# First block of a two-block transformer kernel: stages put in another order, and the context's modulation sums moved from VectorE to GpSimd

## The chip, the cores and the metric

The kernel runs on one core of a Trainium2 chip. The metric is the device time of one execution in microseconds (us). It is one program of about 20,900 instructions; nothing is exchanged with other cores.

## What is computed

Two blocks of a small transformer on 256 tokens of width 1024, all in float32. The first block has two layers; each projects x, forms two attentions (one with low-rank queries and keys, one differential), gates and merges them, and normalises. The second block has half feed-forward sublayers, one windowed attention with a context and one Fourier mixer, and all of them are modulated by vectors that depend only on the inputs `c`, `c_ctx` and `mod_w`:

```python
h = x @ w_in[l]                                   # first block, layer l
y_a = (o_a * silu(gate_a)) @ w_branch_a[l]
y_b = (rms_norm(o_b) * (1 - lam_init) * silu(gate_b)) @ w_branch_b[l]
g = sigmoid(gates + b_merge[l])
merged = g[..., :D] * y_a + g[..., D:] * y_b
x = layer_norm(ALPHA * x + merged @ w_out[l])

mod_lat = silu(c) @ mod_w[i] + mod_b[i]           # second block, sublayers' shift, scale, gate
mod_ctx = silu(c_ctx) @ mod_w[i] + mod_b[i]       # the same for the context, i = 0 only
x = layer_norm(ALPHA * x + gate * y)
```

## The kernel before

**Products in float32.** Every weight piece (128 x 1024, one half of a 1 MB load into one of five raw slots) is split in two: ScalarE writes the rounded part `w_hi` (L1124), VectorE the rest `w_lo` = raw - `w_hi` (`split`, L1488). TensorE multiplies three times for each product (L579 to L581). The activations are split likewise: TensorE transposes, ScalarE writes `xT_hi`, VectorE `xT_lo`. `w_hi` has six slots, so ScalarE and VectorE run at most five to six pieces ahead of TensorE. A piece is 12 matmuls of 128x512 for two token tiles. All order is written by hand: each engine has its own program, and counts in semaphores tie them together. What stands first in an engine's program runs first.

**The first block's layer.** On TensorE: transpose x, ten chunks of `w_in` (the low-rank columns, gate A, then four chunks, later four for the gates), low-rank products, eight heads with one gate piece each, four differential heads with two, the transposes of the gated values, the products with `w_branch_a` and `w_branch_b` (two column halves each, in the banks acc0 to acc3), the transposes of their merged sum, `w_out` in two halves, the second by token tile (`project_by_tile`). VectorE follows with splits, rotations, maxima, gates, and at the end `layer_norm`, which updates, centres and scales tile 0 and then tile 1. `keep_busy(b, n)` issues n needless matmuls (two instructions each, L698) that write a free bank; `turn(..., wait=(5, 10))` puts them ahead of the transposes of each tile.

**The modulation.** The vectors are computed beside this, in chunks of 512 columns. GpSimd's queue loads `mod_w` into a ring of two slots of two features each, `mod_raw` (`mod_load`, L479; four loads a chunk). VectorE multiplies each feature by its `silu` column and adds it to a running sum over eight features (`mod_feature`, L1607 for the first and L1609 for the others). In the first block a chunk is done twice, once for the latents into `mod_sum_lat` (counter `mod_step`) and, in five of six chunks a layer, once for the context into `acc_ctx` (`ctx_step`). TensorE sums over the partitions with `mod_sum` into bank score1, and VectorE's `mod_store` (L1626, L1627) adds the bias and frees the bank. `split_and_mod(n, features)` interleaves n splits with the features. A load waits until VectorE has used the slot before.

**The merge.** VectorE does, for each branch and each half: two splits with a feature, then `products(2)` (wait for TensorE's pieces), then the two gate products (L1815), which free the banks; for the second branch then the sum of both (L1820) and `merged_ready`, one for each half.

**Second block.** `post_norm` multiplies the product by the row `gate_row`. That row is fetched by `gate_load`, which writes the vector of 1024 to DRAM, element by element so that it lies in the order of the columns, and reads it back to all partitions. `project_first` starts a feed-forward by token tile, with `keep_busy` where nothing else is to be done. In `attention`, `pairs` transposes queries and keys through two banks.

Of the kernel before, what the change touches and what calls it, by code (L numbers as in the profile page):

```python
# [21 lines left out]
F32R = mybir.dt.float32r  # L22
# [4 lines left out]
P = 128  # L27
TOK = 256
# [46 lines left out]
MOD_RING = 2  # L75
N_GATES = 7
MOD_KEPT = 3 * D // 512
KEPT_EARLY = 2
SUM_COLS = 48

# [10 lines left out]
FIRST_SPLITS, HEAD_MORE = 1, (1, 3, 5)  # L91
# [45 lines left out]
def program(nc, a, out):  # L137
    with ExitStack() as ctx:
# [19 lines left out]
        x = sb("x", [P, NT, D])  # L158
        xT_hi = sb("xT_hi", [P, KD, TOK], F32R)
        xT_lo = sb("xT_lo", [P, KD, TOK], F32R)  # L160
        mod_raw = sb("mod_raw", [P, MOD_RING, 2, 512])
# [34 lines left out]
        first = ExitStack()  # L196
        scope[0] = first
        low = sb("low", [P, NT, LOW])
        wide = sb("wide", [P, NT, WIDE])
        work = sb("work", [P, 3072])  # L200
        v_a = sb("v_a", [P, NT, HEADS * DV])
        qkT = sb("qkT", [P, 2 * HEADS, TOK])
        qkdT = sb("qkdT", [P, 2 * DHEADS, TOK])
        cT_hi = sb("cT_hi", [P, 3, TOK], F32R)
        cT_lo = sb("cT_lo", [P, 3, TOK], F32R)
        lam_sum = sb("lam_sum", [P, LAYERS * 2])
        low_sq = sb("low_sq", [P, 4])
        low_inv = sb("low_inv", [P, 4])
        row_max = sb("row_max", [P, HEADS, 4])
        neg_max = sb("neg_max", [P, HEADS, 4])  # L210
        row_sum = sb("row_sum", [P, HEADS, 4])
        row_inv = sb("row_inv", [P, HEADS, 4])
        diff_sq = sb("diff_sq", [P, DHEADS * NT])
        diff_inv = sb("diff_inv", [P, DHEADS * NT])
        mod_sum_lat = sb("mod_sum_lat", [P, 512])
        acc_ctx = sb("acc_ctx", [P, 2, 512])
        first.close()

# [10 lines left out]

        second = ExitStack()  # L230
        scope[0] = second
        ctx_area = sb("ctx_area", [P, 2 * 2 * FHALF + NT * 3 * TOK + 12])
        ctx_x = ctx_area[:, 0:NT * D].rearrange("p (t n) -> p t n", t=NT)
        gate_row = sb("gate_row", [P, D])
        turned_more = sb("turned_more", [P, 2, 512])
        gated = sb("gated", [P, NT, D])
        ffn_scope = second.enter_context(ExitStack())
        scope[0] = ffn_scope
        hT_hi = sb("hT_hi", [P, KF, TOK], F32R)
        hT_lo = sb("hT_lo", [P, KF, TOK], F32R)  # L240
        silu_g = sb("silu_g", [P, 2, NT, FC])
        hidden = sb("hidden", [P, 2, NT, FC])
        mod_kept = sb("mod_kept", [P, MOD_KEPT, 512])
        ffn_scope.close()
        att_scope = second.enter_context(ExitStack())
        scope[0] = att_scope
        qkv = sb("qkv", [P, NT, QKV])
        ctx_kv = sb("ctx_kv", [P, NT, 2 * AKV * AD])
        qkv_bias = sb("qkv_bias", [P, QKV])
        ctx_scope = att_scope.enter_context(ExitStack())  # L250
        scope[0] = ctx_scope
        ctxT_hi = sb("ctxT_hi", [P, KD, TOK], F32R)
        ctxT_lo = sb("ctxT_lo", [P, KD, TOK], F32R)
        ctx_scope.close()
        scope[0] = att_scope
        qT = sb("qT", [P, AH // 2, TOK])
        kT = sb("kT", [P, AKV, 2 * TOK])
        band = sb("band", [P, NT, 2 * TOK])
        att_work = sb("att_work", [P, 8 * 512])
        att_max = sb("att_max", [P, AH, NT])  # L260
        att_neg = sb("att_neg", [P, AH, NT])
        att_sum = sb("att_sum", [P, AH, NT])
        att_inv = sb("att_inv", [P, AH, NT])
        sink_exp = sb("sink_exp", [P, AH, NT])
        att_scope.close()
        scope[0] = second
# [1903 lines left out]
```

## Time and profile before

| | |
|---|---|
| median of 3 runs | 1677.95 us (1675.96 to 1678.39) |
| the profiled execution | 1674.37 us |
| its span, first to last instruction | 1672.7 us |
| granted TensorE clock, mean | 0.989 of full |
| busy in the span: TensorE, its weight loads, VectorE, ScalarE, GpSimd | 95%, 79%, 72%, 48%, 8% |
| loads of `mod_w` | 144 of 512 KB, median 6.0 us from issue to landing |
| loads of `b_merge` | 4 of 1024 KB, median 10.1 us |

Times in the profile are in us from the start of the span. A busy TensorE is a model, since its matmuls overlap: 128x512 matmuls are shown with 0.39 us each and start 0.23 us apart. An idle time is put down to the instruction that ended it. "L1609" is a line of the kernel.

### The profile page before, as it was taken

To read this page: it belongs to the slowest core of one execution; us is meant where nothing else is said; L and a number is where in the kernel's file an instruction comes from. 1 tells how busy PE (TensorE), PEld (TensorE's weight loads), DVE (VectorE), ACT (ScalarE), POOL (GpSimd) and SP (SyncE) were. 2 spreads that over 40 slices of the span, in tenths; PEclk is the share of its full clock that TensorE was granted. 3 is DMA by queue.
4 is the path that set the end of the run, shared out by engine and by line. 5 is a ranking of instruction groups with operands and counts; after the bars stand their busy time and mean duration, and the time that the engine had idled before them with its cause. 6 is when DMAs were issued, how large, how long until landed. Compare 5 with 4: busy or idle time off the path is not lost.

```text
span 1672.7 us, 20900 instructions
## 1 busy us (share of the span) xinstructions
PE 1596.4 (95%) x7847; PEld 1318.7 (79%) x7847; DVE 1200.0 (72%) x1847; ACT 794.8 (48%) x1241; POOL 140.3 (8%) x205
## 2 busy tenths in 40 slices
PE   6999989999889999999999799999999999999997
PEld 6887768887778878888888458887888878888876
DVE  6888887987977776777756867777587775566544
ACT  4565534566434444444535465444354443264442
POOL 1100001100001110011100011111001110000000
PEclk9999999999999999999999999999999999999999
DMA  7864357753468877588658205987668866366552
GB/s 266 307 220 154 138 178 267 246 181 132 163 209 263 273 263 246 180 272 284 239 198 240 71 1 181 289 283 266 213 227 278 272 225 232 89 193 195 179 177 76
DMA packets 200509, 349.64 MB, mean 209 GB/s; under 512 B 11188, under 2 KB 128236, under 8 KB 199900
## 3 DMA queue, kind: packets, MB, share of 16 engines
q1 hardware_dynamic: 174668, 252.90, 46.5%
q0 software_dynamic: 25744, 95.43, 16.3%
q8 instruction: 63, 1.03, 0.3%
q14 instruction: 34, 0.28, 0.1%
HBM read 347.21 MB, written 1.08 MB: 208 GB/s over the span
## 4 chain that ended last, share of the span: by engine, by line
PE 82%; DVE 12%; ACT 2%; DMA 2%; issue 1%; SPq 0%; DVEq 0%; ACTq 0%
PE acc L579 24%; PE acc L581 24%; PE acc L580 24%; DVE w_lo L1488 3%; PE turn L923 1%; PE score L706 1%; DMA raw<-in_attn_wqkv 1%; PE acc L831 1%; PE score L1009 1%; DVE x L1589 1%; DVE att_work L2040 1%; DMA raw<-in_w_in 1%; DVE acc_ctx L1609 1%; PE score L718 1%; PE score L698 1%
## 5 line engine op out<-in xcount | busy, mean ns | idle before, releaser
L1488 DVE TENSOR_TENSOR w_lo<-raw,w_hi 128x1024 fp32r<-128x1024 f32 (+2 forms) x490 | 581.4, 1196 | 286.2 <-ACT w_hi L1124 285.2
L1124 ACT ACTIVATE w_hi<-raw 128x1024 fp32r<-128x1024 f32 (+2 forms) x490 | 503.5, 1040 | 505.1 <-PE acc L581 420.8
L579 PE MATMUL acc<-w_hi,xT_hi 128*128 128x512 f32 (+1 forms) x1440 | 573.0, 398 | 17.5 <-DVE wide L1738 6.6
L581 PE MATMUL acc<-w_hi,xT_lo 128*128 128x512 f32 (+1 forms) x1440 | 563.5, 391 | 0.0
L580 PE MATMUL acc<-w_lo,xT_hi 128*128 128x512 f32 (+1 forms) x1440 | 562.6, 391 | 0.0
L579 PEld LDWEIGHTS acc<-w_hi,xT_hi 128*128 128x128 f32 x1440 | 272.3, 189 | 74.0 <-issue 8.4
L581 PEld LDWEIGHTS acc<-w_hi,xT_lo 128*128 128x128 f32 x1440 | 272.2, 189 | 57.2
L580 PEld LDWEIGHTS acc<-w_lo,xT_hi 128*128 128x128 f32 x1440 | 272.5, 189 | 53.1
L479 POOL DMA_DIRECT2D mod_raw<-in_mod_w x144 | 104.3, 724 | 951.9 <-DVE mod_run L1609 758.3
L579 PE MATMUL acc<-w_hi,hT_hi 128*128 128x512 f32 x440 | 174.3, 396 | 0.1
L581 PE MATMUL acc<-w_hi,hT_lo 128*128 128x512 f32 x440 | 173.6, 395 | 0.0
L580 PE MATMUL acc<-w_lo,hT_hi 128*128 128x512 f32 x440 | 173.6, 395 | 0.0
L1609 DVE SCALAR_TENSOR_TENSOR mod_run<-mod_raw,silu_c,mod_run 128x512 f32<-128x512 f32 x216 | 161.2, 746 | 3.8 <-DMA mod_raw<-in_mod_w 3.8
L579 PEld LDWEIGHTS acc<-w_hi,hT_hi 128*128 128x128 f32 x440 | 82.8, 188 | 20.5 <-DVE hT_lo L1950 1.3
L581 PEld LDWEIGHTS acc<-w_hi,hT_lo 128*128 128x128 f32 x440 | 82.8, 188 | 19.5
L580 PEld LDWEIGHTS acc<-w_lo,hT_hi 128*128 128x128 f32 x440 | 82.8, 188 | 19.1
L1355 ACT ACTIVATE silu_g<-acc 128x256 f32<-128x256 f32 x110 | 36.2, 381 | 82.3 <-PE acc L581 82.3
L1188 ACT ACTIVATE turned<-x,neg_mean 128x1024 bf16<-128x1024 f32 x16 | 18.5, 1157 | 85.3 <-DVE neg_mean L1578 85.3
L1609 DVE SCALAR_TENSOR_TENSOR acc_ctx<-mod_raw,silu_c,acc_ctx 128x512 f32<-128x512 f32 x70 | 52.2, 746 | 3.0 <-DMA mod_raw<-in_mod_w 2.9
L1943 DVE TENSOR_TENSOR hidden<-acc,silu_g 128x256 f32<-128x256 f32 x110 | 41.6, 420 | 12.0 <-ACT silu_g L1355 8.1
L1264 ACT ACTIVATE work<-score,neg_max 128x256 f32<-128x256 f32 x64 | 29.6, 472 | 30.5 <-DVE neg_max L1716 30.5
L1950 DVE TENSOR_TENSOR hT_lo<-turn,hT_hi 128x512 fp32r<-128x512 f32 x55 | 38.1, 692 | 3.8 <-ACT hT_hi L1359 3.5
(278 smaller groups left out, 1335.8 us busy)
## 6 DMA issues: line engine op xcount, KB each, us to landing
raw<-in_ffn_wi SPq DMA_DIRECT2D x220, 512.0 KB, 4.9
mod_raw<-in_mod_w POOLq DMA_DIRECT2D x144, 512.0 KB, 6.0
raw<-in_ffn_wo SPq DMA_DIRECT2D x110, 512.0 KB, 4.5
raw<-in_w_in SPq DMA_DIRECT2D x72, 512.0 KB, 7.2
raw<-in_w_out SPq DMA_DIRECT2D x16, 512.0 KB, 4.7
raw<-in_attn_wqkv SPq DMA_DIRECT2D x16, 512.0 KB, 4.7
wide<-in_b_merge POOLq DMA_DIRECT2D x4, 1024.0 KB, 10.1
raw<-in_w_branch_a SPq DMA_DIRECT2D x8, 512.0 KB, 4.6
```

What stands on the lines that cost most here:

```text
L479: pool.dma_start(mod_raw[:, s, :, :], w_mod[l, :, 2 * i:2 * i + 2, at]).then_inc(mod_in[s], 16)
L579: nc.tensor.matmul(dst, xh, wh, start=start, stop=False)
L580: nc.tensor.matmul(dst, xh, wl, start=False, stop=False)
L581: return nc.tensor.matmul(dst, xl, wh, start=False, stop=stop)
L1124: nc.scalar.activation(piece_part(w_hi[:, i % SPLIT_SLOTS, :], i), piece_part(raw[:, s, i % 2 * PIECE:(i % 2 + 1) * PIECE], i), ACT.Copy). ...
L1188: step(nc.scalar.activation(squares[:, t, :], x[:, t, :], ACT.Square, bias=neg_mean[:, t:t + 1], accum_out=square_sum[:, t:t + 1]))
L1264: m = nc.scalar.activation(p[:, t * TOK:t * TOK + TOK], bank[b][:, t * TOK:t * TOK + TOK], ACT.Exp, bias=neg_max[:, h, 2 * m_ + t:2 * m_ + ...
L1355: nc.scalar.activation(silu_g[:, half, t, :], bank[ACC[2 * half + t]][:, FC:2 * FC], ACT.Silu).then_inc(silu_done, 1)
L1488: nc.vector.tensor_tensor(piece_part(w_lo[:, i % RAW_PIECES, :], i), piece_part(raw[:, i // 2 % RAW_SLOTS, i % 2 * PIECE:(i % 2 + 1) * PIE ...
L1609: m = nc.vector.scalar_tensor_tensor(out=end if k == KD - 1 else run, in0=w, scalar=by, in1=run, op0=ALU.mult, op1=ALU.add)
L1943: nc.vector.tensor_tensor(hidden[:, half, t, :], bank[b][:, 0:FC], silu_g[:, half, t, :], ALU.mult).then_inc(moved[b], 1)
L1950: nc.vector.tensor_tensor(sl(hT_lo), bank[b][:], sl(hT_hi).bitcast(F32), ALU.subtract).then_inc(moved[b], 1)
```

## The change

It reorders work of the first block and of the attention, moves buffers within SBUF, and moves one kind of work to another engine.

- The context's features: GpSimd multiplies the loaded weights in place (`tensor_scalar`) and adds them to the running sum (`tensor_tensor`), each followed by a wait for its own end. It does this behind VectorE, which must have read the feature first. A slot is reloaded behind GpSimd's own features. GpSimd's loop over the layers is written out, and the rows and biases of the layer are loaded before the fifth load of the ring, which is now behind the features of the third.
- The merge: products first, splits behind them; the last gate products and the last sum by token tile, with `by_tile` on TensorE's side; the transposes of the merged halves wait separately.
- The layer's end: features in other places, `mod_store` of the fourth chunk ahead of the first early splits, that of the fifth in the wait for the root of the second tile.
- `move_gates` stands ahead of the feature in the heads and ahead of the maxima in the differential heads; `HEAD_MORE` is (1, 4, 5) for (1, 3, 5).
- Fewer `keep_busy`: (0, 6) for (5, 10), and 2, 8, 2 for 6, 11, 6.
- The attention: four banks for the pairs, splits moved behind the copies of the keys and to the last heads, two waits in GpSimd's queue ahead of the loads of the band and of the rows.
- The gate vector is written to DRAM contiguously by partition, and `gate` reads the row with a step of eight elements.

```diff
-FIRST_SPLITS, HEAD_MORE = 1, (1, 3, 5)
+FIRST_SPLITS, HEAD_MORE = 1, (1, 4, 5)
+BRANCH_FEATURES = [(3, 4), (5, 6), (7,), ()]
...
+            def ctx_feature(k):
+                s = k // 2 % MOD_RING
+                if k % 2 == 0:
+                    pool.wait_ge(mod_in[s], 16 * c.next(f"mod_in{s}"))
+                pool.wait_ge(mod_step, c.next("feature") + 2 * MOD_RING)
+                w, by = mod_raw[:, s, k % 2, :], silu_c[:, C_CTX + k:C_CTX + k + 1]
+                if k == 0:
+                    nc.gpsimd.tensor_scalar(acc_ctx[:, 0, :], w, by, None, ALU.mult).then_inc(ctx_step, 1)
+                    pool.wait_ge(ctx_step, c.next("ctx"))
+                    return
+                nc.gpsimd.tensor_scalar(w, w, by, None, ALU.mult).then_inc(ctx_part_ready, 1)
+                pool.wait_ge(ctx_part_ready, c.next("part"))
+                if k == KD - 1:
+                    if c.now("ctx chunk"):
+                        pool.wait_ge(ctx_stored, c.now("ctx chunk"))
+                    c.next("ctx chunk")
+                nc.gpsimd.tensor_tensor(acc_ctx[:, k // (KD - 1), :], w, acc_ctx[:, 0, :], ALU.add).then_inc(ctx_step, 1)
+                pool.wait_ge(ctx_step, c.next("ctx"))
+            def chunk_loads(chunks, behind_first):
+                loads = [(ctx_too, at, i) for ctx_too, at in chunks for i in range(4)]
+                for q in range(len(loads) + MOD_RING):
+                    if q >= MOD_RING:
+                        ctx_too, _, i = loads[q - MOD_RING]
+                        if ctx_too:
+                            for k in (2 * i, 2 * i + 1):
+                                ctx_feature(k)
+                        else:
+                            c.next(f"mod_in{i % MOD_RING}")
+                            c.next("feature", 2)
+                    if q == 4:
+                        behind_first()
+                    if q < len(loads):
+                        _, at, i = loads[q]
+                        s = i % MOD_RING
+                        pool.wait_ge(mod_step, 2 * c.next("mod load"))
+                        pool.dma_start(mod_raw[:, s, :, :], w_mod[0, :, 2 * i:2 * i + 2, at]).then_inc(mod_in[s], 16)
...
+            pool.wait_ge(k_twice_ready, 1)
             pool.dma_start(band[:], a["band"].rearrange("(t p) n -> p t n", p=P)).then_inc(band_in, 16)
+            pool.wait_ge(exps_ready, 1)
             norm_rows(a["ln_g_2"][0, 1], a["ln_b_2"][0, 1])
...
-                after = turn(lambda t, k: x[:, t, k * P:k * P + P], x_tile, wait=(5, 10))
+                after = turn(lambda t, k: x[:, t, k * P:k * P + P], x_tile, wait=(0, 6))
...
+                        if by_tile and t == 0 and i == pieces - 1:
+                            m.then_inc(first_done, 1)
...
-                    split_and_mod(HEAD_PIECES[h], ((h + 3) % KD,), True)
+                    split(HEAD_PIECES[h])
+                    move_gates(HEAD_PIECES[h])
+                    mod_feature((h + 3) % KD)
...
+                for n in range(2):
+                    products(2)
+                    for t in range(NT):
+                        gate_branch(0, n, t)
+                    split_and_mod(2, BRANCH_FEATURES[n])
+                products(2)
+                for t in range(NT):
+                    gate_branch(1, 0, t)
+                dve.wait_ge(moved["acc1"], c.next("acc1 moved", 13) + 1)
+                for t in range(NT):
+                    m = merge(0, t)
+                m.then_inc(merged_ready, 1)
+                split_and_mod(1, BRANCH_FEATURES[2])
+                for t in range(NT):
+                    if t == 0:
+                        dve.wait_ge(first_done, c.next("first"))
+                    else:
                         products(2)
+                    b = ACC[2 + t]
+                    gate_branch(1, 1, t)
+                    dve.wait_ge(moved[b], c.next(b + " moved", 11 - 4 * t) + 1)
+                    merge(1, t).then_inc(merged_ready, 1)
                 c.next("acc1 moved")
                 turn_plain(xT_hi, xT_lo, scale=0.5)
-                split_and_mod(2, range(0, 4), True)
-                mod_store(*ctx_chunk(3))
-                split_and_mod(1, range(4, 6), True)
+                split_and_mod(3, BRANCH_FEATURES[3])
+                split_and_mod(2, range(0, 4))
+                split_and_mod(1, range(4, 7))
...
+                mod_store(*ctx_chunk(3))
                 split(EARLY)
-                for k in (6, 7):
-                    mod_feature(k, True)
-                layer_norm(update, lambda t: wide[:, t, 0:D], between=split)
-                mod_store(*ctx_chunk(4))
+                mod_feature(7)
+                layer_norm(update, lambda t: wide[:, t, 0:D], between=split, at_root=lambda: mod_store(*ctx_chunk(4)))
                 mods_stored()
...
-                    nc.vector.scalar_tensor_tensor(out=gated[:, t, at], in0=bank[b][:], scalar=factor, in1=gate_row[:, at],
+                    by_chunk = lambda r: r.rearrange("q (k p) -> q k p", p=P)
+                    row = gate_row[:].rearrange("q (p k) -> q k p", k=KD)[:, 4 * n:4 * n + 4, :]
+                    nc.vector.scalar_tensor_tensor(out=by_chunk(gated[:, t, at]), in0=by_chunk(bank[b][:]), scalar=factor, in1=row,
                                                    op0=ALU.mult, op1=ALU.mult).then_inc(moved[b], 1)
```

## Rows read from the trace of the kernel before

**Rows 1.** Busy time in the first layer; columns: PE, PEld, DVE, ACT, POOL, clock, DMA
```profile
21.68:257.68 236.00, 219.42 (x1159) 187.43 (x1159) 193.84 (x356) 120.20 (x229) 19.53 (x28) 0.97 0.59 198
```
**Rows 2.** TensorE's waits in the whole span: us in total, times, longest
```profile
PE score L600 <- DVE mod_lat L1627: 8.6, 2, 4.4
PE acc L579 <- DVE wide L1738: 6.6, 4, 2.0
...
PE score L600 <- DVE wide L1820: 5.7, 2, 3.6
...
PE acc L579 <- DVE wide L1815: 4.2, 2, 2.1
```
**Rows 3.** Timeline of TensorE behind the merge: start, us, line, operation, [idle before]
```profile
221.12 0.63 PE L580 MATMUL acc<-w_lo,xT_hi 128*128 128x512 f32 x1
221.55 0.53 PE L581 MATMUL acc<-w_hi,xT_lo 128*128 128x512 f32 x1
221.91 0.39 PE L579 MATMUL acc<-w_hi,xT_hi 128*128 128x512 f32 x1
222.15 0.40 PE L580 MATMUL acc<-w_lo,xT_hi 128*128 128x512 f32 x1
```
**Rows 4.** Timeline of TensorE at the end of the first layer
```profile
243.51 0.99 PE L706 MATMUL score<-ones,mod_sum_lat 128*128 128x48 f32 x8
...
251.55 0.44 PE L600 MATMUL score<-ident,x 128*128 128x128 f32 x2 [4.18 <-DVE mod_lat L1627]
251.83 3.81 PE L698 MATMUL acc<-ones,ident 128*128 128x128 f32 x20
255.43 0.87 PE L600 MATMUL turn<-ident,x 128*128 128x128 f32 x4
...
257.68 0.43 PE L579 MATMUL acc<-w_hi,xT_hi 128*128 128x416 f32 x1
```
**Rows 5.** Timeline of VectorE at the end of the first layer
```profile
247.29 0.68 DVE L1833 SCALAR_TENSOR_TENSOR x<-x,acc 128x512 f32<-128x512 f32 x1
...
250.07 1.28 DVE L1589 SCALAR_TENSOR_TENSOR x<-wide,inv_std,ln_rows 128x1024 f32<-128x1024 f32 x1
```
**Rows 6.** Timeline of VectorE in the attention, behind the keys
```profile
935.54 3.49 DVE L1488 TENSOR_TENSOR w_lo<-raw,w_hi 128x1024 fp32r<-128x1024 f32 x3
```
**Rows 7.** Timeline of TensorE: first pairs of the attention; filler of `project_first`
```profile
935.68 3.44 PE L991 MATMUL turn<-ident,qkv 128*128 128x128 f32 x16 [3.67 <-DVE gated L2014]
...
1028.06 2.62 PE L698 MATMUL score<-ones,ident 128*128 128x128 f32 x22
```
**Rows 8.** VectorE's groups in the first layer: count, busy us, mean ns, idle before
```profile
L1488 DVE TENSOR_TENSOR w_lo<-raw,w_hi 128x1024 fp32r<-128x1024 f32 (+3 forms) x64 | 70.6, 1115 | 6.9 <-ACT w_hi L1124 6.6
...
L1609 DVE SCALAR_TENSOR_TENSOR acc_ctx<-mod_raw,silu_c,acc_ctx 128x512 f32<-128x512 f32 x35 | 26.1, 746 | 2.5 <-DMA mod_raw<-in_mod_w 2.5
...
L1607 DVE TENSOR_SCALAR acc_ctx<-mod_raw,silu_c 128x512 f32<-128x512 f32 x5 | 2.4, 483 | 2.8 <-DMA mod_raw<-in_mod_w 2.8
```
**Rows 9.** GpSimd's arithmetic by line: duration in ns, least, median, most
```profile
L530 POOL TENSOR_TENSOR xT_lo<-gated,xT_hi x8: 727/732/740, 959.7 to 1006.0; 128x256 fp32r<-128x256 f32 x8
...
L528 POOL CAST xT_hi<-gated x8: 392/398/1323, 959.2 to 1004.6; 128x256 fp32r<-128x256 f32 x8
```
**Rows 10.** Timeline of GpSimd's queue: biases, then the fifth load of the ring
```profile
36.51 1.11 POOL L506 DMA_DIRECT2D wide<-in_b_merge  x2
...
41.14 0.72 POOL L479 DMA_DIRECT2D mod_raw<-in_mod_w  x1 [2.48 <-DVE mod_run L1609]
```
**Rows 11.** Timeline of VectorE: the first feature of the second chunk
```profile
54.90 0.49 DVE L1607 TENSOR_SCALAR acc_ctx<-mod_raw,silu_c 128x512 f32<-128x512 f32 x1 [2.76 <-DMA mod_raw<-in_mod_w]
```
**Rows 12.** Timeline of TensorE: `mod_sum` of the second chunk
```profile
78.75 0.99 PE L706 MATMUL score<-ones,mod_sum_lat 128*128 128x48 f32 x8
```
**Rows 13.** Timelines of VectorE and GpSimd where both read SBUF
```profile
1004.47 1.22 DVE L1488 TENSOR_TENSOR w_lo<-raw,w_hi 128x1024 fp32r<-128x1024 f32 x1
...
1004.62 1.32 POOL L528 CAST xT_hi<-gated 128x256 fp32r<-128x256 f32 x1 [4.03 <-DVE gated L2066]
```

More of the change, by code:

```diff
@@ new lines, in program @@
+        mod_sum_lat = sb("mod_sum_lat", [P, 512])
+        acc_ctx = sb("acc_ctx", [P, 2, 512])
+        first.close()
+        scope[0] = ctx
+        second = ExitStack()
+        scope[0] = second
+        ffn_scope = second.enter_context(ExitStack())
+        scope[0] = ffn_scope
+        hT_hi = sb("hT_hi", [P, KF, TOK], F32R)
+        hT_lo = sb("hT_lo", [P, KF, TOK], F32R)
+        silu_g = sb("silu_g", [P, 2, NT, FC])
+        hidden = sb("hidden", [P, 2, NT, FC])
+        mod_kept = sb("mod_kept", [P, MOD_KEPT, 512])
@@ L227, in program @@
         rot = turned[:, 0:2, 0:HEADS * ROPE]
[L230 to L266, printed above, removed]
-        xmT = sb("xmT", [P, KD, TOK])
-        spectrum = sb("spectrum", [P, NT, FGROUPS, 2 * FHALF])
-        second.close()
         dft_ch = ctx_area[:, 0:4 * FHALF].rearrange("p (k n) -> p k n", k=2)
@@ L672, in project_by_tile, with project @@
                         m.then_inc(first_done, 1)
-            def project(banks, pieces, k0=0, n=512, after=None, xh=xT_hi, xl=xT_lo, ready=None):
+            def project(banks, pieces, k0=0, n=512, after=None, xh=xT_hi, xl=xT_lo, ready=None, by_tile=False):
                 dst = [take(b) for b in banks]
@@ L890, in _ @@
                 diff_values(DHEADS - 1)
+                after = turn(lambda t, k: wide[:, t, GATE_A + k * P:GATE_A + k * P + P], groups=range(2))
                 mod_sum(True)
-                after = turn(lambda t, k: wide[:, t, GATE_A + k * P:GATE_A + k * P + P], groups=range(2))
                 project(ACC[0:2], 2, k0=0, after=after)
@@ L1097, in fourier @@
                 project_by_tile(ACC[2:4])
-            after = turn_x(wait=(5, 10))
+            after = turn_x(wait=(0, 6))
             keep_busy("acc0", 5)
@@ new lines, in merge @@
+                def merge(n, t):
+                    of = lambda branch: wide[:, t, GATES + branch * D + n * 512:GATES + branch * D + n * 512 + 512]
+                    return nc.vector.tensor_tensor(of(0), of(0), of(1), ALU.add)
+                for n in range(2):
[6 more added lines that the diff above has]
+                    gate_branch(1, 0, t)
@@ L2034, in attention @@
                         c.next(b)
+                split()
                 def maxima(h):
```

205 lines of the change are left out of this document (114 added, 91 removed).

## Prediction

> **What bounds the kernel now.** I read the page first: TensorE is busy 95% of the span, so a gain can come only from stretches where it stands or runs slowly. The window of the first block's first layer [rows 1] shows where they are: of 236.0 us TensorE is busy 219.4, VectorE 193.8 (82%), GpSimd 19.5. Next the list of TensorE's waits [rows 2]: the four entries that the change touches are all on VectorE and all in the first block: 8.6 + 6.6 + 5.7 + 4.2 = 25.1 us over the two layers. The half-feed-forward stages of the second block hardly appear in that list, and the change leaves their order alone. So the question is the first block and, less, the attention.
>
> Then the timelines. In the merge of the two branches TensorE waits for `wide` L1815, because VectorE does two splits and two features ahead of the product that frees the bank, and for `wide` L1820 at the end. Behind such a wait its matmuls start 0.43 us apart instead of 0.23, at the lower of the two clocks (1.2 GHz): [rows 3] show the end of such a stretch. At the end of a layer [rows 4] TensorE waits 4.18 us for `mod_lat` L1627 (the bank score1, which `mod_store` empties only behind the layer norm), then runs 20 filler instructions for 3.81 us although `x` was ready at 251.35 [rows 5], and resumes real work at 257.68.
>
> **The reordering, part by part.** (1) Merge. `products` and the gate products now stand ahead of the splits, so the wait for L1815 goes: 4.2 us. The last gate products go tile by tile with `by_tile`; tile 0 is finished while TensorE is still on tile 1 (six matmuls of 0.23, 1.4 us), so behind the last matmul only one gate product and one sum are left, about 1.3 us, of which 1.0 lies beside transposes. I leave 0.45 us of each of the two waits for L1820: 5.7 - 0.9 = 4.8 us. The cold stretch has about nine matmuls at 0.2 us extra, 1.8 us, and comes once in each layer: 3.6 us. Sum 12.6.
>
> (2) Ends of layers. VectorE loses features ahead of the first update, which is queued behind them now. TensorE has the first tile finished at about 238.0 (half of its 48 matmuls of 0.23 before 243.5), so that update can begin there; the second tile's update cannot begin before the last matmul at 243.5, it begins at 247.29 now, so `x` is ready about 3.8 us sooner, at 247.5. `mod_store` moves into the wait for the root, so score1 is free in time. The filler ahead of the second tile falls from 20 instructions to 12 (1.6 us at full clock) and ends near 247.8. From the transposes of the second tile (255.43) to the resumption (257.68) is 2.25 us [rows 4]; 247.8 + 2.25 = 250.05 against 257.68 is 7.6 us. The other layer end has the same wait (8.6 less 4.18 is 4.4) and the same fillers; I take 7.5 there, 15.1 in all. At the very start the same fillers are cut, but there ScalarE waits for weights, so I count nothing.
>
> (3) Attention. One split ahead of the rotation of the keys goes away, and two of three behind it [rows 6]: 3.49/3 = 1.16 each, 3.5 us in a chain on which TensorE waits 3.67 [rows 7] and again further on. Four banks for the pairs instead of two add nothing, ScalarE and VectorE empty them at the old pace. The wait put ahead of the band's load holds GpSimd, and behind it the rows of the norm and the gate; the band's 512 KB then arrive about when the first maxima want them, so I take 2.5 of the 3.5. With `project_first` the filler falls from 12 and 22 instructions to 4 and 16, and 12 to 4; it stands ahead of transposes whose input is ready, and 22 of it take 2.62 us [rows 7]: some 0.9 us twice in each of two calls, 3.6. Sum 6.1.
>
> (4) Heads. 6.6 us of waits for `wide` L1738 [rows 2]: `move_gates` now precedes the feature and the extra split of head 3 goes to head 4. All of it could go; with GpSimd on the same memory I take 2.
>
> (5) The gate vector goes to DRAM contiguously, and `gate` reads its row with a step of eight elements. The cheaper transfer is hidden already. What the stepped read costs VectorE no row shows: between nothing and doubling a 0.7 us instruction (the sum of 512 elements of [rows 5] is 0.68), some eight of them with nothing beside them, 0 to 5 us. I take 0, the second input being one of two and the first from PSUM, and keep 5 for the range.
>
> Together 12.6 + 15.1 + 6.1 + 2 = 35.8 us. The moves of buffers in SBUF cost nothing by themselves.
>
> **GpSimd's features.** Off VectorE come, per layer, 35 instructions of 0.746 and five of 0.483, 26.1 + 2.4 = 28.5 us of the 193.8 [rows 1, 8]. On GpSimd each becomes a multiply and an add of 128x512. The trace has its cast and add at 128x256, 0.40 and 0.73 us [rows 9]; a feature is thus between 1.13 (if size cost nothing) and 2.26 (double). The step from the cast to the add shows that time per element matters more than a fixed part, so I stay near double, 2.0: 35 x 2.0 + 5 x 0.7 = 73.5 us per layer, on an engine busy for 19.5 of 236. In itself that fits. Two things don't come free.
>
> First the ring of two slots. A slot is now reloaded only when VectorE and then GpSimd have read it, and GpSimd works in place. Now the loads of the biases go out at 36.5 and the fifth load at 41.14 [rows 10], and VectorE gets it at 54.90, after a wait of 2.76 [rows 11]: these transfers are already late. In the change the biases stand behind GpSimd's features of the third load, which VectorE cannot touch before some 38; with 4 us for two features and a lag, they go out at about 43 to 44, and the first feature of the second chunk comes at 60 to 62. VectorE's splits stand in order behind it; TensorE has a lead of about two pieces there, so it is caught once. Then a slot's turn is load 6.5 (the page's median for it is 6.0, and these stretches are crowded) + VectorE 2.5 + GpSimd 2.5 = 11.5 for two pairs of features, 5.75 each, where TensorE asks for a pair in 5.5 (two pieces of 12 matmuls of 0.23), hence no catching up, and `mod_sum(True)`, which TensorE reaches at 78.75 [rows 12], must wait for GpSimd's last add near 83 to 85. I price this at 5 to 8 us per layer, 6.5 taken: 13 for the two. The bounds are 0 (the load lands as before) and 12 per layer.
>
> Second the memory port. One pair of rows speaks of it: VectorE's split, both inputs in SBUF, starts at 1004.47 for 1.22; GpSimd's cast starts at 1004.62 and lasts 1.32 instead of 0.40, ending 0.25 after the split [rows 9, 13]. So GpSimd stands while VectorE has such an instruction. Whether VectorE stands for GpSimd no row shows. I take a little, 3 us in all, because in the dense stretches both read all the time.
>
> The Trainium skill (SBUF — State Buffer, section Who interferes with whom) says that a VectorE instruction with two SBUF inputs and a GpSimd instruction that reads SBUF exclude one another, whichever starts second blocking for the whole of the other. [Rows 13] agree for the one direction. By that rule the other direction holds too, and the sum would be that of rival B below.
>
> Sum: 35.8 - 13 - 3 = about 20 us. The profiled execution took 1674.4 (span 1672.7, 1.7 around it), 3.6 below the median of the runs shown, 1677.95. 1674.4 - 20 is 1654.4 there, and 1658 on the median's level: I forecast 1657.
>
> **Rivals.** A: GpSimd's work is free, its loads come in time: -36, that is 1642. For it: GpSimd is idle 90% and TensorE's lead is five pieces; against it: [rows 10, 11]. Chance 0.20. B, slower: VectorE pays for GpSimd's port. Per layer VectorE then has 193.8 - 28.5 + 73.5 = 238.8 us against 236.0 for the whole layer now, and it still has to wait for TensorE and ScalarE at least 10 us: 249 per layer, 13 more than now, times two is 26, less 6 for attention: 20 slower, 1698. It decides from the point where VectorE's paid time reaches about half of GpSimd's 73.5: there a layer needs 202 + 20 to 30 of dependency waits and the gain of the reordering is used up. For it: the splits and the latents' 40 or more features, two SBUF inputs each, are 70.6 and some 30 us per layer [rows 8]; against it: a third of VectorE's work reads PSUM, and only one direction is seen. Chance 0.19, half of it below 1690. C: the stalls move from the ends of layers to the ring one for one, 12 per layer and port 9: within 0.2%, or 3 us, of now. Chance 0.07. The forecast's own case, 1646 to 1668, has 0.54.
>
> **Numbers.** Likeliest case 1657, its own range 1646 to 1668. For 8 in 10: down to A's 1640, up into B's lower half, with the 5 us of the stepped read, 1688. Faster by over 0.2% (3.4 us, about what a measurement can tell from no change): 0.54 + 0.20 = 0.74; same 0.07; slower 0.19.
>
> **What would show it.** In the changed trace: no wait of TensorE for the gate product of `wide` (now L1815), under 1 us for the merged sum (now L1820); a layer end that resumes about 7 us after the last `mod_sum`; a new wait of TensorE for `acc_ctx` or for a split early in each layer, and of VectorE for `mod_raw` there. If VectorE's splits are longer than 1.22 us, or its instructions start late, while GpSimd is at a feature, B holds. Splits of constant length and GpSimd's instructions stretched in places mean that only GpSimd pays. The prediction is wrong if a feature takes GpSimd over 3 us, or if VectorE is blocked for over 20 us per layer.

## The result: 57 us slower, and where they are in the profile after

The changed kernel takes 1734.37 us (1734.28 to 1737.24, 4 runs) against 1677.72 (1675.96 to 1678.39, 4 runs): ratio 1.0343, 95% interval 1.0326 to 1.0361. The forecast was 1657. Times of experiments below are medians; the kernel before had medians of 1675.1 to 1678.5 beside them.

The page of the kernel after, its busy line and its clock by slices (in tenths of full speed):

```profile
span 1732.6 us, 20738 instructions
...
PE 1603.5 (93%) x7749; PEld 1330.3 (77%) x7749; DVE 1211.7 (70%) x1766; ACT 794.6 (46%) x1241; POOL 403.8 (23%) x355
...
PEclk9889988889988999999999999999999999999999
```

Start with the stage. VectorE's last scaling of x in the first block, then the last of all, in the kernel before (its own rows, not among those above):

```profile
484.15 1.28 DVE L1589 SCALAR_TENSOR_TENSOR x<-wide,inv_std,ln_rows 128x1024 f32<-128x1024 f32 x1
...
1668.34 1.28 DVE L1589 SCALAR_TENSOR_TENSOR x<-gated,inv_std,ln_rows 128x1024 f32<-128x1024 f32 x1
```

and in the kernel after:

```profile
555.69 1.29 DVE L1651 SCALAR_TENSOR_TENSOR x<-wide,inv_std,ln_rows 128x1024 f32<-128x1024 f32 x1
...
1728.25 1.29 DVE L1651 SCALAR_TENSOR_TENSOR x<-gated,inv_std,ln_rows 128x1024 f32<-128x1024 f32 x1
```

The first block ends 71.5 us later; from there to the end it is 1172.6 us against 1184.2, so 11.6 us sooner. The whole loss is in the first block, where the modulation runs. TensorE's waits there are new:

```profile
PE score L767 <- POOL acc_ctx L529: 34.5, 3, 12.0
PE score L767 <- issue: 26.2, 3, 9.5
PE turn L657 <- DVE wide L1873: 10.5, 2, 5.3
...
PE score L657 <- DVE wide L1873: 6.8, 4, 2.3
```

Six times in ten chunks TensorE stands some 10 us in front of `mod_sum`, 60.7 us in all. The first two lines are one cause: "issue" is a wait for which no releaser is recorded, and the timeline has GpSimd's last addition right before it. TensorE's and then GpSimd's rows, second chunk of the first layer:

```profile
95.06 1.91 PE L767 MATMUL score<-ones,mod_sum_lat 128*128 128x48 f32 x8 [9.53 <-issue]
```

```profile
64.13 2.97 POOL L520 TENSOR_SCALAR acc_ctx<-mod_raw,silu_c 128x512 f32<-128x512 f32 x1 [4.61 <-DVE mod_run L1665]
...
70.98 0.76 POOL L551 DMA_DIRECT2D mod_raw<-in_mod_w  x1 [0.30 <-POOL acc_ctx L529]
71.79 2.01 POOL L523 TENSOR_SCALAR mod_raw<-mod_raw,silu_c 128x512 f32<-128x512 f32 x1
73.89 1.28 POOL L529 TENSOR_TENSOR acc_ctx<-mod_raw,acc_ctx 128x512 f32<-128x512 f32 x1
75.27 1.57 POOL L523 TENSOR_SCALAR mod_raw<-mod_raw,silu_c 128x512 f32<-128x512 f32 x1
76.92 2.05 POOL L529 TENSOR_TENSOR acc_ctx<-mod_raw,acc_ctx 128x512 f32<-128x512 f32 x1
79.27 0.76 POOL L551 DMA_DIRECT2D mod_raw<-in_mod_w  x1 [0.30 <-POOL acc_ctx L529]
...
87.48 0.76 POOL L551 DMA_DIRECT2D mod_raw<-in_mod_w  x1 [0.30 <-POOL acc_ctx L529]
...
93.39 1.57 POOL L529 TENSOR_TENSOR acc_ctx<-mod_raw,acc_ctx 128x512 f32<-128x512 f32 x1
```

GpSimd never rests here for more than 0.3 us: one load and two features take it 8.3 and 8.2 us. TensorE wants two features in 5.5. The last addition ends at 94.96 and TensorE goes on at 95.06. It comes back at the lower clock: the granted clock is 1.00 in the 5 us ahead of the wait and 0.50 in the 5 us behind it, and the eight small matmuls take 1.91 us, 0.99 in [rows 12]. Over the stretch of [rows 1] the granted clock is 0.91 now instead of 0.97.

VectorE stands for the same reason on the other side, since a slot is reloaded only behind GpSimd. Its waits for `mod_raw`:

```profile
DVE mod_run L1667 <- DMA mod_raw<-in_mod_w: 78.5, 21, 9.1
...
DVE mod_run L1665 <- DMA mod_raw<-in_mod_w: 25.1, 4, 11.5
```

Where both engines work, GpSimd holds VectorE up in a second way. GpSimd's rows, then VectorE's:

```profile
45.30 1.56 POOL L523 TENSOR_SCALAR mod_raw<-mod_raw,silu_c 128x512 f32<-128x512 f32 x1
46.95 1.34 POOL L529 TENSOR_TENSOR acc_ctx<-mod_raw,acc_ctx 128x512 f32<-128x512 f32 x1
```

```profile
46.39 0.75 DVE L1667 SCALAR_TENSOR_TENSOR mod_run<-mod_raw,silu_c,mod_run 128x512 f32<-128x512 f32 x1 [3.98 <-DMA mod_raw<-in_mod_w]
47.06 2.31 DVE L1550 TENSOR_TENSOR w_lo<-raw,w_hi 128x1024 fp32r<-128x1024 f32 x1
```

The feature begins inside GpSimd's multiplication and takes its usual 0.75 us; the split begins inside the addition and takes 2.31 us instead of 1.22. The first block's timeline has the same throughout, counted over its rows of one instruction. Of 29 features and splits that begin inside an addition, 26 are longer, by 0.97 us on average; the other three begin in its last 0.06 us. Of 67 that begin inside a multiplication, 53 keep their length, and the others grow by 0.43 us at most.

### The profile page after: what moved, and what is told of

It reads as the page before. It is cut to its first block, busy times and chain, and to the rows that moved or that the text cites. A ratio compares the mean times of both kernels' runs of the same rounds, so it can differ in the third digit from the quotient of the medians.

```text
span 1732.6 us, 20738 instructions
## 1 busy us (share of the span) xinstructions
PE 1603.5 (93%) x7749; PEld 1330.3 (77%) x7749; DVE 1211.7 (70%) x1766; ACT 794.6 (46%) x1241; POOL 403.8 (23%) x355
## 4 chain that ended last, share of the span: by engine, by line
PE 68%; DVE 7%; POOL 5%; DMA 1%; ACT 1%; issue 1%; POOLq 0%; DVEq 0%; ACTq 0%
PE acc L636 20%; PE acc L638 20%; PE acc L637 20%; POOL mod_raw L523 2%; POOL acc_ctx L529 2%; PE turn L986 1%; DVE w_lo L1550 1%; DMA mod_raw<-in_mod_w 1%; DVE gated L1971 1%; PE score L779 1%; PE score L1072 1%; DVE att_work L2115 1%; PE score L767 1%; PE acc L892 1%; DVE x L1977 1%
## 5 line engine op out<-in xcount | busy, mean ns | idle before, releaser
L1550 DVE TENSOR_TENSOR w_lo<-raw,w_hi 128x1024 fp32r<-128x1024 f32 (+2 forms) x490 | 591.1, 1213 | 267.5 <-ACT w_hi L1187 267.0
L1667 DVE SCALAR_TENSOR_TENSOR mod_run<-mod_raw,silu_c,mod_run 128x512 f32<-128x512 f32 x216 | 180.3, 835 | 78.8 <-DMA mod_raw<-in_mod_w 78.5
L490 POOL DMA_DIRECT2D mod_raw<-in_mod_w x96 | 69.4, 723 | 536.0 <-DVE mod_run L1667 434.1
L523 POOL TENSOR_SCALAR mod_raw<-mod_raw,silu_c 128x512 f32<-128x512 f32 x70 | 131.6, 1880 | 134.3 <-DVE mod_run L1667 125.0
L529 POOL TENSOR_TENSOR acc_ctx<-mod_raw,acc_ctx 128x512 f32<-128x512 f32 x70 | 104.8, 1498 | 5.8
L638 PEld LDWEIGHTS acc<-w_hi,hT_lo 128*128 128x128 f32 x440 | 82.6, 188 | 17.3
L767 PE MATMUL score<-ones,mod_sum_lat 128*128 128x48 f32 x96 | 17.4, 340 | 60.7 <-POOL acc_ctx L529 34.5
L767 PEld LDWEIGHTS score<-ones,mod_sum_lat 128*128 128x128 f32 x96 | 16.7, 260 | 63.2 <-issue 63.1
```

The source lines that it names most:

```text
L490: pool.dma_start(mod_raw[:, s, :, :], w_mod[l, :, 2 * i:2 * i + 2, at]).then_inc(mod_in[s], 16)
L523: nc.gpsimd.tensor_scalar(w, w, by, None, ALU.mult).then_inc(ctx_part_ready, 1)
L529: nc.gpsimd.tensor_tensor(acc_ctx[:, k // (KD - 1), :], w, acc_ctx[:, 0, :], ALU.add).then_inc(ctx_step, 1)
L638: return nc.tensor.matmul(dst, xl, wh, start=False, stop=stop)
L767: m = nc.tensor.matmul(dst[:, 4 * i + j:4 * i + j + SUM_COLS], acc[:, j * P:j * P + P], ones[:, 0:SUM_COLS], start=True, stop=True)
L1550: nc.vector.tensor_tensor(piece_part(w_lo[:, i % RAW_PIECES, :], i), piece_part(raw[:, i // 2 % RAW_SLOTS, i % 2 * PIECE:(i % 2 + 1) * PIE ...
```

## Experiments: which half of the change it is

**Each half alone.** E1 is the changed kernel with `mod_feature(k, True)` back on VectorE; E2 is the kernel before with only the context's features and their loads on GpSimd.

```diff
-                split_and_mod(8, range(8))            # E1, and so for every call
+                split_and_mod(8, range(8), True)
```

> The changed kernel with the context's features back on VectorE; the order, the fillers, the banks, the places of the buffers and the gate row stay as changed. Theory W (GpSimd's features cost the time, because loads, VectorE's features and the partition sum wait for them; the reordering does what was forecast): 1640 to 1650, TensorE's waits for the partition sum gone. Rival R (a good part of the 57 us comes from the reordering itself, such as the fillers cut or the stepped read of the gate row): 1665 or more.

> The kernel before with one thing changed: the context's features of the first block on GpSimd, with the loads behind them, as in the change. Theory W: slower than before by 80 to 100 us (the 57 of the change plus some 35 that the reordering gives), 1760 to 1775. Rival R: 1700 to 1735, since then the two halves add up the other way.

E1: 1649.62 us, ratio 0.983 (0.981 to 0.985), 27 us faster than before. E2: 1752.21, ratio 1.044 (1.042 to 1.046). The move to GpSimd costs 75 us alone and 84.8 on top of the reordering; the reordering gives 27, not 35.8. E2 lies between its two expectations, so the halves do not simply add: on top of the move the reordering is worth only 18 us (1752.2 less 1734.4). E2 has the same waits at `mod_sum` in the old order, six with 58.0 us in all, so they come from the move and not from the reordering.

**Waits or sizes.** E3 keeps every instruction, wait and load and lets GpSimd work on 32 of the 512 columns. E4 keeps the sizes, takes `acc_ctx` as the only data and issues each load ahead of the features, so that no slot waits for GpSimd.

```diff
-                nc.gpsimd.tensor_scalar(w, w, by, None, ALU.mult).then_inc(ctx_part_ready, 1)
+                nc.gpsimd.tensor_scalar(w[:, 0:32], w[:, 0:32], by, None, ALU.mult).then_inc(ctx_part_ready, 1)
```

> The changed kernel with GpSimd's multiplies and adds on 32 of the 512 columns; the rest of the context's modulation is left out. All waits, counts and the order of the queue stay. Theory W, with the duration as its cause: about as the first kernel of this call, 1640 to 1655, and VectorE's wait for loads under 20 us in the block. Rival S (the chain of semaphores, loads behind features, whatever their duration): over 1690. Theory P (VectorE pays for GpSimd's port) can't be told from W here.

> The changed kernel with GpSimd's features at full size, but reading and writing only acc_ctx instead of the loaded weights (so the context's modulation is not computed), and each load issued ahead of the features of the load before last. The loads no longer wait for GpSimd to finish with a slot. If the ring is the cause (reload behind GpSimd): VectorE's waits for mod_raw fall from 104 us to under 40 and the time to about 1670. If GpSimd's rate is the cause (over 3 us a feature against 2.7 us a piece): the sums still wait about 10 us each and the time stays above 1700.

E3: 1649.08 us (two runs), as E1. With a quick GpSimd the 85 us are gone, though every semaphore, shared slot and late load is still there, and TensorE's waits at `mod_sum` fall from 60.7 to 0.7 us. The chain is not free for all that. VectorE still waits 58.6 us for `mod_raw`, where under 20 were expected, and E3 only equals E1, although it has taken the context's features off VectorE; E13 below shows some 17 us that this could give. E4: 1710.4 (two runs, 1705.8 and 1715.0), 24.0 less than the changed kernel, with 51.6 us of waits at `mod_sum` left: mostly the rate, and the ring has its share. With two runs 9 us apart, the 24.0 is known to a few us only.

**Nobody waits for the sums.** E6 is E4 without TensorE's wait; TensorE sums `mod_sum_lat` twice instead.

```diff
-                if ctx_too:
-                    pe.wait_ge(ctx_step, c.next("ctx mod", 8))
```

> The run with other data (1710.4 us), and now nobody waits for GpSimd's sums: TensorE's mod_sum doesn't wait for them and sums mod_sum_lat a second time in place of acc_ctx. GpSimd issues the same instructions on the same amount of data; the context's modulation is not computed. Theory W (GpSimd is too slow for the dense chunks, TensorE waits for its last addition): the 51.6 us of waits at mod_sum go, 1658 to 1670. Theory P (VectorE pays for the shared memory port): the time hardly falls, 1690 or more.

1685.55 us (1681.2 to 1689.9, 10 runs). The 51.6 us of waits are gone and 24.8 us are gained. Neither theory alone: 36 us above E3 remain, in which nobody waits for a result of GpSimd.

**The port.** This is short for whatever makes VectorE and GpSimd wait for each other when both read SBUF. E10 is E6 with GpSimd about as long at a feature but on 32 columns at a time; E13 is E6 with memsets, which write and read nothing.

```diff
+                for m in range(3):                    # E10, the multiply; the add twice
+                    o = nc.gpsimd.tensor_scalar(part(m), part(m), by, None, ALU.mult)
```

> The run in which nobody waits for GpSimd (1685.6 us), with each 128x512 multiply replaced by three of 128x32 and each add by two of 128x32: GpSimd is as long at a feature (3 x 0.84 + 2 x 0.37 = 3.3 us by the run with 32 columns) but moves less than a quarter of the data. The context's modulation is not computed. Theory P (what is left against the run with 32 columns, 36 us, is VectorE blocked by GpSimd's large accesses: its features took 0.97 us there and 0.75 here): 1648 to 1655, and VectorE's features at 0.75. Theory Q (it is GpSimd's time at a feature, behind which its queue issues the loads late): 1675 to 1690.

> The run in which nobody waits for GpSimd (1685.6 us), with each multiply and each add replaced by two memsets of 128x512, which write SBUF and read nothing. The context's modulation is not computed. Theory R (only instructions of GpSimd that read SBUF exclude VectorE): VectorE's features stay at 0.75 us while GpSimd is busy, 1648 to 1660. Theory X (writes exclude it as well): VectorE's features at 0.9 or more, above 1665 if the memsets take GpSimd as long.

VectorE's latent features in the first 500 us, in E6, E10 and E13 in turn (count, busy us, mean ns, idle before):

```profile
L1663 DVE SCALAR_TENSOR_TENSOR mod_run<-mod_raw,silu_c,mod_run 128x512 f32<-128x512 f32 x72 | 69.7, 968 | 40.0 <-DMA mod_raw<-in_mod_w 39.7
```

```profile
L1664 DVE SCALAR_TENSOR_TENSOR mod_run<-mod_raw,silu_c,mod_run 128x512 f32<-128x512 f32 x72 | 54.5, 757 | 51.7 <-DMA mod_raw<-in_mod_w 51.4
```

```profile
L1661 DVE SCALAR_TENSOR_TENSOR mod_run<-mod_raw,silu_c,mod_run 128x512 f32<-128x512 f32 x80 | 59.8, 748 | 18.4 <-DMA mod_raw<-in_mod_w 18.1
```

E10: 1668.56 us, between the theories. VectorE's features fall from 968 to 757 ns, 15.2 us over these 72, and 17.0 us are gained. That gain is not VectorE's price at the port alone, for GpSimd is also 46 us shorter in all (203 against 249). What is left against E13 would be GpSimd's own time, with its queue late with the loads; that is argued, not shown, for VectorE's waits for `mod_raw` do not follow the times: 58.6 us in E3, 65.2 in E6, 75.6 in E10, 28.9 in E13. GpSimd in E10 pays at the port as well: six small multiplies took 5.31 us where three took 1.03 elsewhere,

```profile
60.63 5.31 POOL L519 TENSOR_SCALAR acc_ctx<-acc_ctx,silu_c 128x32 f32<-128x32 f32 x6
...
71.06 1.03 POOL L519 TENSOR_SCALAR acc_ctx<-acc_ctx,silu_c 128x32 f32<-128x32 f32 x3
```

E13: 1632.31 us (one run), below both theories; four memsets also take only 2.1 us where a feature took 3.2. They stay at 0.53 us each and VectorE at 748 ns: memsets, which only write, disturb nobody. E13 is also the nearest that these runs come to a free move: with the context's features off VectorE and nobody waiting, E1 would gain about 17.3 us. So the 84.8 us are 24.0 (the slots) + 24.8 (TensorE's wait) + 17.0 (smaller accesses: VectorE at the port and a shorter GpSimd, not told apart) + 36.3 (GpSimd's length, its own stretching at the port and the late loads, not told apart) - 17.3. The order of the steps matters: in E3, with short instructions, slots, waits and port together leave the kernel only 16.8 us above E13.

The Trainium skill (SBUF — State Buffer, section Who interferes with whom) says that a VectorE instruction with two SBUF inputs contends with a GpSimd instruction that reads SBUF and not with one that only writes. The runs agree: 968 ns in E6, 748 in E13, and the split of 2.31 us above is the direction that no row before showed. They add which instruction it is, for the multiplication reads SBUF too, and 53 of the 67 VectorE instructions that began inside one were not held up.

**Where work is sparse.** E9 is E1 with one chunk of five on GpSimd, the one in the heads.

> The kernel with all of the reordering and the context's features on VectorE (1649.6 us), but one of the five context chunks of each layer, the one in the differential rotation and the heads, is on GpSimd as in the change (two instructions a feature, 3.3 us). There VectorE asks for one feature per head, every 7 to 9 us. Theory W (only GpSimd's rate in the dense chunks costs): 1645 to 1652, no wait of TensorE at this chunk's mod_sum over 1 us. Theory P (each feature on GpSimd costs by the port or the slots, wherever it is): a fifth of the 85 us, 1662 or more.

1658.94 us (1650.2 to 1661.3), between the two expectations: 9.3 slower than E1, where a fifth of 85 is 17. The profiled execution was its fastest, 1650.23, and has no wait at this `mod_sum`. What the slower ones paid stays open.

## Experiments: the parts of the reordering

Each undoes one part of E1 (1649.62).

```diff
-                    row = gate_row[:].rearrange("q (p k) -> q k p", k=KD)[:, 4 * n:4 * n + 4, :]
+                    row = gate_row[:, at]             # E5, with the old store of the vector
```

> The kernel with all of the reordering and the context's features on VectorE (1649.6 us), with one part undone: the gate row is stored element by element and read contiguously again. In that kernel the 28 gate products take 1.107 us each, against 0.685 in the kernel before: 11.8 us more of VectorE. Theory P (the stepped read is paid on the path): one or two of the gate products of the second tile stand on the path in each of seven normalisations, 0.42 each, so 3 to 6 us less: 1644 to 1647. Theory H (it is hidden, as the prediction took it, or the slow store takes the gain back): 1649 to 1651.

E5: 1640.82 us, **8.8 faster**, more than either theory had. The gate products of the kernel after tell why (least, median and most, ns):

```profile
L1971 DVE SCALAR_TENSOR_TENSOR gated<-acc,gate_row x28: 1057/1119/1146, 745.4 to 1723.9; 128x512 f32<-128x512 f32 x28
```

A row read with a step of eight elements costs 1.11 us, 0.685 without it: 28 times 0.42 are 11.8, and what E5 gains is three quarters of that.

> The kernel with all of the reordering and the context's features on VectorE (1649.6 us), with one part undone: the needless matmuls are as many as before (5 and 10 ahead of the transposes of x, and 6, 11, 6 in project_first). The prediction put 1.6 us of filler in each layer's end and 3.6 in the attention. Theory F (fillers stand ahead of ready work): 4 to 8 us more, 1654 to 1658. Theory N (they fill waits that are there anyway, or what they cost comes back by a higher clock): 1648 to 1652.

> The kernel with all of the reordering and the context's features on VectorE (1649.6 us), with the order of the heads undone: feature ahead of move_gates, maxima ahead of move_gates in the differential heads, the extra split in head 3. The prediction took 2 us for this part; the stretch between the low-rank norm and the end of the heads became shorter by 3.8 and 5.4 us in the traces. Theory G (the heads are worth what the stretch shows): 1656 to 1660. Theory K (2 us, and the rest comes from what is done elsewhere): 1650 to 1653.

> The kernel with all of the reordering and the context's features on VectorE (1649.6 us), with the attention undone: two banks for the pairs, one split ahead of the rotation and three behind it, no waits ahead of the loads of the band and the rows. The fillers stay as in the change. The prediction took 2.5 us for this part and 3.6 for the fillers; the stretch of the attention became 9.3 us shorter in the traces, and the fillers turned out to be worth nothing. Theory B (splits and banks are worth it all): 1657 to 1660. Theory K (2.5 us): 1651 to 1653.

E8 (all fillers, the `keep_busy` matmuls, as before): 1650.38, nothing. E11 (heads): 1660.28, so they are worth 10.7; the four waits for the gate's sum are back as in [rows 2] (6.6 us). E12 (attention): 1653.51, 3.9.

> The kernel with all of the reordering and the context's features on VectorE (1649.6 us), with the merge undone: two splits and a feature stand ahead of each pair of gate products again, both sums of a half are made together, and TensorE's last product isn't told by token tile. The prediction put 12.6 us on this part (4.2 and 4.8 of waits, 3.6 of the low clock). Theory M (as predicted): 1660 to 1663. Theory D (the wait for the first gate product goes, the wait for the merged sums only splits in two, and the clock falls all the same, as the trace shows): some 2 us in each layer, 1652 to 1655.

> The kernel with all of the reordering and the context's features on VectorE (1649.6 us), with the layer's end undone except its fillers: features 6 and 7 behind the early splits, mod_store of the fourth chunk between the splits, that of the fifth behind the norm. The prediction put 15.1 us on this part. Theory M (as predicted, less the fillers): 1658 or more. Theory D (only mod_store inside the root's wait matters, since the last update began no sooner in the trace): TensorE's waits for mod_lat come back, 3 to 4 us in each layer, 1655 to 1658. Theory O (it is nothing): 1648 to 1652.

E14: 1641.24 us, **8.4 faster**, against both theories: the new merge costs where it was to gain 12.6. E15: 1649.46, nothing, although TensorE's waits for `mod_lat` double (8.6 us against 4.3 in E1). VectorE's rows of E1, behind the differential norm, show a hole of 4.34 us, where the kernel before had 1.32 (at 194.56):

```profile
184.41 0.15 DVE L1662 TENSOR_TENSOR mod_lat<-score,modb 128x4 f32<-128x4 f32 x1
188.90 0.43 DVE L1570 CAST xT_hi<-turned 128x512 fp32r<-128x512 f32 x1 [4.34 <-ACT turned L1196]
```

Features 3 and 4 used to stand in it. `BRANCH_FEATURES` moved them between the splits, where VectorE sets the pace. E17 puts only them back:

```diff
+                for k in (3, 4):
+                    mod_feature(k, True)
                 for g in range(2):
```

> The kernel with all of the reordering and the context's features on VectorE (1649.6 us), with one part of the merge undone: features 3 and 4 stand ahead of the scaled transposes again, where VectorE waits for ScalarE, not between the splits; the order of products, gate products and splits stays as changed. VectorE waits there for 4.34 us without them, and for 1.67 with them in the run with the merge undone (1641.2 us). Theory G (the 8.4 us that the undone merge gained are these two features, 3.0 us of VectorE in each layer moved out of idle time into a stretch where VectorE sets the pace): 1641 to 1645. Theory O (it is the order of products and splits): 1648 to 1650.

```profile
185.75 0.74 DVE L1644 SCALAR_TENSOR_TENSOR mod_run<-mod_raw,silu_c,mod_run 128x512 f32<-128x512 f32 x1
188.21 0.43 DVE L1570 CAST xT_hi<-turned 128x512 fp32r<-128x512 f32 x1 [1.71 <-ACT turned L1196]
```

1639.74 us, better than expected: the two features are the whole of it, and the new order of products and splits by itself gains nothing.

> The reordering without its merge and without the stepped row, the context's features on VectorE. If the gains of the two runs add up, 1649.6 - 8.4 - 8.8 = 1632 us; if the second is partly the first once more, up to 1637.

> As the kernel with the two features in the gap, and the row stored element by element and read contiguously. Theory G: 1632 to 1637, no slower than the run with the whole merge undone, so that the merge's new order is worth between 0 and 4 us by itself. Theory O: 1639 to 1641.

> The kernel with neither the new merge nor the stepped row, the context's features on VectorE (1631.2 us), and now the end of the first block's layers undone as well: features, mod_store and the fillers ahead of x as before. Undone in the kernel with the misplaced features, features and mod_store gave nothing (1649.5 against 1649.6), and the fillers nothing (1650.4). Theory M (the layer's end is worth something, but there the misplaced features held VectorE back, so that the last update was late either way): from the end of the last products to the ready x VectorE is 3.6 us per layer faster than before in the trace, and the transposes no longer wait for mod_lat: 1637 to 1646. Theory O (it is nothing anywhere): 1630 to 1633.

**E16: 1631.16 us, ratio 0.973 (0.971 to 0.975), is the fastest kernel of this study**, 45 us faster than the kernel before; the two gains add up. E18: 1634.79 (0.974 to 0.978), 3.6 slower, with intervals that just overlap: the new merge order gains nothing and may cost a little. E19 undoes the layer's end on E16, fillers too: 1646.24, **15.1 slower**, where on E1 neither the layer's end (E15) nor the fillers (E8) gave anything. A wait of TensorE in E19:

```profile
PE score L631 <- DVE mod_lat L1660: 8.6, 2, 4.4
```

The wait for `mod_lat` is back as in [rows 2]; in E16 it is 2.5. The end of the first layer on TensorE, from the last `mod_sum` to the next real work, in E16 and then in E19:

```profile
238.16 0.99 PE L739 MATMUL score<-ones,mod_sum_lat 128*128 128x48 f32 x8
...
244.77 0.43 PE L610 MATMUL acc<-w_hi,xT_hi 128*128 128x416 f32 x1
```

```profile
236.16 0.99 PE L739 MATMUL score<-ones,mod_sum_lat 128*128 128x48 f32 x8
...
250.35 0.43 PE L610 MATMUL acc<-w_hi,xT_hi 128*128 128x416 f32 x1
```

That is 6.6 us against 14.2, so 7.6 less; at the end of the second layer it is 10.8 against 15.4. VectorE begins the update of the second tile 0.4 us behind that `mod_sum` in E16 and 3.8 behind it in E19, as in the kernel before. In E1 it begins 4.8 us behind and in E17 still 2.8. So with the new merge VectorE comes late to the layer's end, and the two misplaced features are a part of that. It would explain why E15 gains and loses nothing; no run shows it alone.

## Why the prediction was wrong, step by step

- **GpSimd's feature, the step that decided.** The prediction took 2.0 us, reasoned from a cast and an add of 128x256 [rows 9]. It measured 3.38, over the 3 us that the prediction itself named as the sign of being wrong. The rows of the kernel after:

```profile
L523 POOL TENSOR_SCALAR mod_raw<-mod_raw,silu_c 128x512 f32<-128x512 f32 x70 | 131.6, 1880 | 134.3 <-DVE mod_run L1667 125.0 <-DVE mod_sum_lat L1667 5.3
L529 POOL TENSOR_TENSOR acc_ctx<-mod_raw,acc_ctx 128x512 f32<-128x512 f32 x70 | 104.8, 1498 | 5.8
...
L520 POOL TENSOR_SCALAR acc_ctx<-mod_raw,silu_c 128x512 f32<-128x512 f32 x10 | 28.1, 2813 | 50.4 <-DVE mod_run L1665 50.4
```

  A feature takes 1.88 + 1.50 = 3.38 us on average, 2.85 where nothing stretches it (1.57 + 1.28), a first one 2.81 instead of 0.7. The upper bound of 2.26 was none: it doubled the cast's 0.40, but the multiply is another instruction and takes 1.57; and the stretching that [rows 13] show was charged to VectorE alone, not to GpSimd's length.
- **Ring and last add.** Mechanism right, size wrong. Biases at 43 to 44: 48.58. First feature of the second chunk at 60 to 62: 63.46. Last add at 83 to 85: 94.96. With 3.4 us a feature a pair of them takes 8.2 us of GpSimd alone, not 5.75 with the load in it, so TensorE is caught three times a layer, not once: 30 us of waits per layer instead of 6.5. The price was worked out once for one chunk and the bound of 12 inherited the 2.0.
- **Port.** 3 us forecast. E10 bounds what VectorE pays at about 17, so rival B's mechanism, which the cited rule named, is real in both directions. How much of the loss is the port in all is open: GpSimd's own stretching, 3.38 us a feature against 2.85, is port too and no run takes it out alone. Rival B's 1698 is passed with TensorE's waits, which it left out: without them E6 takes 1685.6. Rival A's 1642 is 10 above the 1632 that a GpSimd without reads gives.
- **Merge, +12.6.** Wrong sign: -8.4 with features on VectorE. L1815's wait did go, but that for the merged sum grew from 5.7 [rows 2] to 8.1 in E1 and 17.3 in the kernel after, and the features moved out of an idle gap weren't priced at all. The clock falls as before: the granted clock of the 19 us around this wait is 0.91 in E1 and in the kernel before.
- **Ends of layers, +15.1.** Mechanism and size right, once VectorE is in time: E19 measures 15.1 (17.6 by the two ratios). The first layer's end resumes 6.6 us behind the last `mod_sum` in E16 and gains the 7.6 forecast, and the update begins 3.4 us sooner where 3.8 were said. The second gains 4.7 instead of 7.5, so the exact 15.1 is luck in part: some 3 us of it lie elsewhere. In the changed kernel the merge before it spoils the gain.
- **Attention and its fillers, 6.1.** 3.9 and nothing for the fillers. **Heads, 2 of 6.6.** 10.7, more than all of the 6.6: the whole of the waits was the better guess, and what the other 4 us are was not told apart.
- **Stepped read, 0 of 0 to 5.** 8.8. "The second input being one of two" was a hope, not a row.
- **Sum of the reordering.** 27 instead of 35.8. Undone one at a time, the good parts give 10.7 + 3.9 (both on E1) + 15.1 (on E16) = 29.7 of the 45 us of E16; the remaining 15 were not told apart.

## What to carry to other kernels

Before work moves to an idle engine, time the very instruction there at full size, contention included, and divide: if its time per item is above what the consumer asks for in the densest stretch, the busy share of the whole span says nothing. Work that can be done at any time belongs in an engine's idle gaps, where it waits for another engine. Moved into a stretch that the engine itself paces, it can cost more than its length: 9.9 us here for four instructions of 3.0 us together in each of two layers. A part that gains nothing when undone alone may be hidden behind another part's loss; undo it again on the repaired kernel.

## What the hardware showed that was not expected

- GpSimd's multiply by a column, 128x512 in float32, takes 1.56 to 1.58 us where nothing stretches it, and the add 1.26 to 1.29 (kernel after); a multiply of 128x32 takes 0.36 in the median, three in a row 1.03 (E10).
- VectorE and GpSimd stretch each other in both directions when both read SBUF: VectorE's feature goes from 0.746 to 0.968 us on average (E6), a split up to 2.31 (kernel after). It is GpSimd's addition that holds VectorE, 26 times out of 29 and nearly to its end; its multiplication did so 14 times out of 67, for 0.43 us at most (kernel after). Memsets by GpSimd, 0.53 us for 128x512, do neither (E13).
- A VectorE instruction with one input from PSUM and the other read from SBUF with a step of 32 bytes takes 1.11 us instead of 0.685 (E1 and E5). The Trainium skill (SBUF — State Buffer, section Door 1: The DMA port swizzle) says that consecutive accesses within one line of 16 bytes get full bandwidth and that each step to a new line pays; the rows agree, with a factor of 1.62 for this one step; no other step was measured.
